# Moving the add of the shift rows in both MoE token stages from VectorE to GpSimd, and one step of ScalarE's order

## The reference, cut to what matters

```python
def rms_norm(x, g):
    xf = x.astype(jnp.float32)
    y = xf * lax.rsqrt(jnp.mean(xf * xf, axis=-1, keepdims=True) + EPS)
    return (y * g.astype(jnp.float32)).astype(x.dtype)

def modulate(h, shift, scale):
    return h * (1 + scale) + shift

for l in range(DEPTH):
    ...
    x = x + g1 * y_x                                            # after the token mixers and w_out
    hx2 = modulate(rms_norm(x, norm_ffn_g[l]), sh2, sc2)        # the token rows of this case
    x = x + g2 * grouped_moe(hx2, router_w, router_b, w_exp_gate[l], w_exp_up[l], w_exp_down[l])
    ...                                                         # the same for the context tokens in layer 0
return rms_norm(x, final_g)
```

## Time and profile before

| | |
|---|---|
| median of the runs | 1579.54 us (3 runs, 1579.3 to 1580.94) |
| profiled execution, own time | 1578.25 us |
| its span | 1576.6 us |
| TensorE busy | 1506.4 us (96%) |
| VectorE busy | 704.4 us (45%) |
| ScalarE busy | 332.8 us (21%) |
| GpSimd busy | 118.8 us (8%) |
| DMA read and written | 361.66 MB and 12.98 MB, 238 GB/s over the span |
| mean granted TensorE clock | 0.986 of full |

### The profile page before, as it was taken

How to read it: one execution, slowest core, us unless ns; L and a number is a source line. 1 busy time by engine, 2 the same in 40 slices (tenths; PEclk the granted TensorE clock), 3 DMA queues, 4 the chain that set the end, 5 groups by cost and what they waited for, 6 DMA issues and landing times. The chain is left out here.

```text
span 1576.6 us, 23833 instructions
## 1 busy us (share of the span) xinstructions
PE 1506.4 (96%) x9898; PEld 1023.3 (65%) x9898; DVE 704.4 (45%) x1420; ACT 332.8 (21%) x769; POOL 118.8 (8%) x101
## 2 busy tenths in 40 slices
PE   5999999999999999899999999999999999899995
PEld 2765644766677768775546648786678887655563
DVE  1497777577775442732221135336534312512122
ACT  2121244322223110210101023225322211100001
POOL 0100000032212210000000030000000000000000
PEclk9999999999999999999999999999999999999998
DMA  9575411333544589489999984431134376899997
GB/s 372 203 239 166 156 54 43 119 133 124 158 147 160 173 286 358 173 322 391 400 394 392 402 314 147 138 97 45 38 111 146 121 283 266 343 426 428 419 411 296
DMA packets 128364, 370.24 MB, mean 235 GB/s; under 512 B 14269, under 2 KB 91351, under 8 KB 107516
## 3 DMA queue, kind: packets, MB, share of 16 engines
q1 hardware_dynamic: 118588, 344.86, 58.8%
q10 hardware_dynamic: 5936, 13.09, 2.3%
q0 software_dynamic: 3728, 10.71, 1.9%
HBM read 361.66 MB, written 12.98 MB: 238 GB/s over the span
## 5 line engine op out<-in xcount | busy, mean ns | idle before, releaser
L1247 PE MATMUL ps<-hT,ring 128*128 128x512 f32 (+1 forms) x544 | 207.6, 535 | 0.0
L1250 PE MATMUL ps<-ring,hT 128*128 128x256 f32 (+1 forms) x832 | 173.1, 364 | 3.7 <-DVE arena L2242 2.3
L1250 PEld LDWEIGHTS ps<-ring,hT 128*128 128x128 f32 x832 | 147.0, 190 | 27.5 <-issue 10.3
L1247 PEld LDWEIGHTS ps<-hT,ring 128*128 128x128 f32 x544 | 101.3, 191 | 86.9 <-issue 81.7
L1446 PE MATMUL ps<-arena,ring 128*128 128x512 f32 (+1 forms) x384 | 136.3, 486 | 0.0
L1596 PE MATMUL ps<-arena 128*32 128x128 f32 (+2 forms) x1104 | 102.4, 342 | 0.7 <-DVE arena L2554 0.7
L1596 PE MATMUL ps<-ring,arena 128*64 128x256 f32 (+1 forms) x1280 | 93.9, 334 | 3.8 <-DMA ring<-in_w_exp_gate 2.1
L1446 PEld LDWEIGHTS ps<-arena,ring 128*128 128x128 f32 x384 | 72.4, 190 | 31.7 <-issue 24.6
L2856 POOL DMA_INDIRECT arena<-moe_rows,idx_i x23 | 22.8, 991 | 897.8 <-DVE idx_i L2622 512.9
L1381 PE MATMUL ps<-hT,ring 128*128 128x256 f32 x384 | 87.9, 379 | 0.6 <-ACT arena L1903 0.6
L1159 PE MATMUL ps<-ring,arena 128*128 128x256 f32 x384 | 85.9, 380 | 2.5 <-DVE arena L2420 2.5
(11 more groups left out here) (310 smaller groups left out, 1962.5 us busy)
## 6 DMA issues: line engine op xcount, KB each, us to landing
ring<-in_w_in SPq DMA_DIRECT2D x54, 1024.0 KB, 6.2
ring<-in_w_ada SPq DMA_DIRECT2D x48, 1024.0 KB, 5.3
arena<-in_w_exp_down SPq DMA_DIRECT2D x18, 2048.0 KB, 16.1
arena<-in_w_exp_up SPq DMA_DIRECT2D x15, 2048.0 KB, 15.8
ring<-in_w_exp_down SPq DMA_DIRECT2D x14, 2048.0 KB, 13.7
ring<-in_w_exp_gate SPq DMA_DIRECT2D x12, 2048.0 KB, 16.4
ring<-in_w_exp_up SPq DMA_DIRECT2D x12, 2048.0 KB, 15.0
hT<-in_w_exp_gate SPq DMA_DIRECT2D x10, 2048.0 KB, 15.7
```

What stands on the lines that cost most here:

```text
L1247: last = pe.matmul(ps[:, bank, 0:tok.stop - tok.start], w[:, k, at:at + width], hT[:, k, tok], start=(k == 0), stop=(k == KD - 1))
L1250: last = pe.matmul(ps[:, bank, 0:width], hT[:, k, P * tok:P * (tok + 1)], w[:, k, at:at + width], start=(k == 0), stop=(k == KD - 1))
```

## The change

GpSimd makes the adds of the shift rows: `shift_rows` moves from VectorE's list to GpSimd's, in front of the gathers of each layer. Its input no longer comes from `mix_tmp` for all tiles: the scaled rows of tile `t` go to the place of tile `t` + 1 in `h_toks`, and only those of the last tile to `mix_tmp`. VectorE counts each finished tile of scaled rows in the semaphore `consts_made` (which had stood at 4 by then), and GpSimd waits for that, and for its own add of the tile before, which reads the place that it is about to write. VectorE no longer waits for the add before `mix`; it waits for all adds of the layer only in `order_experts`, whose scratch space `by_place` begins where `mix_tmp` lies. On ScalarE `keep_parts(t - 1)` stands ahead of the squares of tile `t`, where it had stood behind them.

```diff
+CONSTS = 4
...
+        def rows_scaled(l, t):
+            return h_toks[l][:, t + 1, :] if t < NT - 1 else mix_tmp
...
                 for t in range(t0, NT):
-                    squares(ready, junk2, t, t + 1)
                     if t > t0:
                         keep_parts(t - 1)
+                    squares(ready, junk2, t, t + 1)
                 keep_parts(NT - 1)
...
                 def scale_rows(t, half):
                     cols = slice(512 * half, 512 * (half + 1))
-                    step(dve.scalar_tensor_tensor(out=mix_tmp[:, cols], in0=res[:, t, cols], scalar=rstd[:, t:t + 1],
-                                                  in1=ffn_rows[l][t // XT][0][:, cols], op0=ALU.mult, op1=ALU.mult))
-
-                def shift_rows(t):
-                    by_row = lambda a: a.rearrange("p (q k) -> p q k", k=KD)
-                    dve.tensor_tensor(h_toks[l][:, t, :].rearrange("p (k q) -> p q k", k=KD), by_row(mix_tmp),
-                                      by_row(ffn_rows[l][t // XT][1]), ALU.add).then_inc(h2_ready, 1)
+                    ins = dve.scalar_tensor_tensor(out=rows_scaled(l, t)[:, cols], in0=res[:, t, cols], scalar=rstd[:, t:t + 1],
+                                                   in1=ffn_rows[l][t // XT][0][:, cols], op0=ALU.mult, op1=ALU.mult)
+                    if half:
+                        ins.then_inc(consts_made, 1)
...
                     if v >= 2:
                         dve.wait_ge(x_mixed, v - 1)
-                    if half and t > t0:
-                        dve.wait_ge(h2_ready, before(nq, l) + t - t0)
...
                     scale_rows(t, 1)
-                    if t < NT - 1:
-                        shift_rows(t)
...
                                          op0=ALU.is_lt, op1=ALU.mult).then_inc(assigned, 1)
-                shift_rows(NT - 1)
...
                 def order_experts():
                     step(dve.tensor_tensor(versus, bc(rank[:, :].unsqueeze(1), *pair), bc(e_num.unsqueeze(2), *pair), ALU.is_equal))
                     by_number = by_place[:, 0, :, :]
+                    dve.wait_ge(h2_ready, before(nq, l + 1))
...
+            def shift_rows(l, t):
+
+                by_row = lambda a: a.rearrange("p (q k) -> p q k", k=KD)
+                if t > first_tile(l):
+                    pool.wait_ge(h2_ready, before(nq, l) + t - first_tile(l))
+                pool.wait_ge(consts_made, CONSTS + before(nq, l) + t - first_tile(l) + 1)
+                pool.tensor_tensor(h_toks[l][:, t, :].rearrange("p (k q) -> p q k", k=KD), by_row(rows_scaled(l, t)),
+                                   by_row(ffn_rows[l][t // XT][1]), ALU.add).then_inc(h2_ready, 1)
+
             for l in range(DEPTH):
                 pool.dma_start(list_d.rearrange("(p n) o -> p (n o)", p=P), no_token[:, :]).then_inc(zeroed, 16)
+                for t in range(first_tile(l), NT):
+                    shift_rows(l, t)
                 pool.wait_ge(next_idx, nth_list(l, 1))
```

More of the change, by code:

```diff
@@ L458, in trunk @@
         rows_zeroed, mods_row = sem("rows_zeroed"), sem("mods_row_ready")
-        consts_made = sem("consts_made")
+        consts_made = sem("consts_made_then_rows_scaled")
         cols_turned, cols_kept = sem("cols_turned_then_sums_of_quarters"), sem("cols_kept_then_exps_of_constants")
```

## The result

The changed kernel takes 1583.45 us (median of 11 runs, 1582.12 to 1584.54), the kernel before 1580.19 (11 runs, 1579.3 to 1580.94). The ratio is 1.0019, with a 95% interval of 1.0011 to 1.0027: **slower by about 3 us**, where 2.8 us less was forecast. The profiled execution of the changed kernel took 1584.54 us, the longest of its 11, and that of the kernel before took 1578.25, less than any of its 11 runs here; so the 6.2 us between their spans are more than the difference of the medians. The two already stand 2.5 us apart when the stage of layer 0 begins (the first product of the second half is taken up at 632.43 instead of 629.94), though nothing is changed ahead of it, and 0.9 us at that place of layer 1. I take these two offsets out where I say so. What makes them wasn't looked for.

A forecast was written before the change was run, and what follows sets the result against it. The last expert weights' DMA was taken to bound the end, TensorE the chain before. Gains of 0.8 us in layer 0 and 2.0 in layer 1 made 2.8 us off the 1579.54 median: 1576.7 us, range 1572.5 to 1581.0.

The forecast's parts named there:

- the layer 1 term: Layer 1: `first_rows` starts 1.5 us earlier, the load waiting for TensorE follows, and the weight stream gains about 2.0 us.
- rival 1: Layer 1: TensorE's 2 us idle keeps the clock low over `first_rows`, costing 2.5 us; total 1579.2 us; chance 0.2.
- GpSimd's add: Shift-row add of one tile, 1024 columns with reordered write: taken as 2.35 us, other end 3.74 us.
- rival 4: Both layers: the reordered write stretches GpSimd's add to 3.74 us; total 1580.8 us, 1583.5 with a low clock; chance 0.16.
- The hold: Chain to the choice, both layers: GpSimd's add blocks VectorE's operations reading two SBUF operands, taking about 2.2 us.
- Rival 3: Both layers: VectorE isn't held, or only for a moment, keeping about 2.2 us each; total 1572.3 us; chance 0.08.
- The tile loop's 0.93 us: First tile, once in each layer: TensorE's router no longer waits for VectorE's copy of the transposed rows, 0.93 us gained.
- ScalarE's 0.85 us: Last tile's router: kept parts copied ahead of the squares remove a wait of 1.02 us, counted as 0.85 us gained.
- The first rows of layer 0: Behind the choice in layer 0: `first_rows` starts 0.8 us earlier, passing whole to the end of the layer.
- Rival 2: Layer 0: the clock is high over `first_rows`, 3.2 us more gained; total 1573.5 us; chance 0.12.
- The hole at 1347: DMA standstill, 1347 to 1351.5 us: the load of 1351.36 goes at 1346.5 and fills it, leaving a shorter one later.
- The residual add of layer 1: Second tile, on VectorE: held by GpSimd's add, over 0.9 us long, ending about 1340.0 instead of 1340.86.

The follow-up runs named there:

- The best kernel here: Changed kernel, each layer's last-tile add back on VectorE, 18 `keep_busy` matmuls before the choice, 8 instead of 3 behind the places: 1575.13 us, ratio 0.9962.
- the run with 17: Changed kernel with each layer's last-tile add back on VectorE and 17 instead of 10 `keep_busy` matmuls in each layer: 1578.50 us, ratio 0.9982.

## Why the prediction was wrong

**The step that failed** is the layer 1 term, 2.0 us gained, and in it the words "the load after it waits for TensorE, 1.5 us earlier than 1358.99". It took the clock over `first_rows` as the kernel before has it, though the text had just worked out that the fillers now end 2 us before the choice. That case was set aside as rival 1 with a chance of 0.2 and 2.5 us. It is what happened, in both profiles of the changed kernel, and it costs 5.5 us at the release of the load: 13.1 us instead of 7.65 for the three groups, since not only the first part of the first rows but the second part and most of the first gate weights too ran at 1.2 GHz (until 1363.3). The prediction's own sign of being wrong, a clock of 0.50 over `first_rows` of layer 1, is there. With 5.5 instead of 2.5 and the rest as forecast, rival 1 would have given 1582.2 us, outside the stated range but near the measured 1583.45. The experiment with four fillers in the kernel before shows the mechanism without the change, the one with 22 in the changed kernel takes it away. Counted from where VectorE takes up the first product of layer 1's second half, the load goes after 27.92 and 27.93 us in the two profiles of the kernel before, after 32.53 and 31.20 in the two of the changed kernel, after 33.62 with four fillers in the kernel before, and after 26.31 with 22 in the changed one. That last one is 1.6 us earlier than in the kernel before, as forecast (1.5), and that kernel takes 0.20% less (0.11 to 0.28), where 0.18% was forecast. So the rest of the sum came to about the right size once the clock was high; that it agrees so closely is in part luck, since the fillers of layer 0 were changed too.

**Point by point.**

- GpSimd's add: 2.35 us taken, 2.37 measured. The reordered write costs GpSimd next to nothing (2367 ns against 2352), so rival 4 is out, which took 3.74. The ratio of the Trainium skill ("GPSIMD Engine Reference", elementwise cycle accounting), applied to VectorE's 1.94 us, would have had 3.8. The trace differs from that use of it: 2.37 / 1.94 is 1.22.
- The hold: right in kind and size (2.1 us in both layers, on a comparison of 0.2 us). Rival 3 is out. A short operation that reaches the port first does not help, as L2564 shows: the next one is held.
- The tile loop's 0.93 us: right, in both layers. ScalarE's 0.85 us: near in the profile (1.02 less 0.29 is 0.73), though as a change of its own it can't be seen in the time.
- The first rows of layer 0, forecast 0.8 us earlier: 668.66 - 666.77 less the offset of 2.49 is 0.6 earlier. The missing 0.2 are the three fillers behind the count, which at 1.2 GHz take 1.63 us instead of 0.91 and end last. The same in layer 1: 0.87 earlier instead of 1.5. This is a second, small step that failed: I let VectorE's marks end that wait and didn't look at what stands ahead of `first_rows` on TensorE's own list. It too comes from the low clock.
- Rival 2, a better clock in layer 0: not shown. The first part took 6.03 us in the first profile and 5.65 in the second, but in the kernel before it took 6.98 in one and 5.44 in the other, so the two kernels can't be told apart here.
- The hole at 1347 filled, and another in its place: right in kind, but it was to be shorter than the first, and it is 5 us. The 1.5 us from issue to the first data, part of the 2.0 us of layer 1, is too long where the queue is empty: behind the load of 1364.51 the DMA engines move nothing until 1365.4 and are at work by 1365.6, about 1 us after the issue. No run shows the 2.0 us as such, since the spans follow the load behind TensorE alone.
- The residual add of layer 1, forecast to be held to 1340.0 and to take over 0.9 us: it ended at 1340.83, which is 0.9 us earlier than before once the offset of 0.91 is taken off, as forecast (0.86), but it took 0.78 us. The end is right by luck. VectorE waited 0.89 us for TensorE's product before it, and the add started at 1340.05, when GpSimd's had only 0.25 us to go.

## What to carry to other kernels

Where an engine waits for a short chain on others, a microsecond moved off that chain isn't gained until you have looked at what TensorE does meanwhile: ten fillers took 2.48 us here with the clock high and 4.61 with it low, so the same number of them covers a wait in one execution and leaves a gap in the next. The best kernel here had them sized for 2.4 GHz and for the longest wait, on both sides of a short burst of real work. There is a price: where the clock is low, as many of them end behind the choice (by 2.1 us with 17 in the kernel before). Look at several profiles. And an operation put on GpSimd beside VectorE was not parallel to it while both read two operands from SBUF (2.33 us instead of 0.2), while VectorE's copy out of PSUM beside it took 0.68 us, against 0.67 in the kernel before: put it where VectorE works out of PSUM or waits, not beside the chain that everybody waits for.

## What the hardware showed that I had not expected

GpSimd's reordered write (neighbours 512 bytes apart) is all but free, 2367 ns against 2352, where VectorE takes 1.94 us with the same pattern and 1.22 without it. TensorE stayed at 1.2 GHz for 20.7 us in the changed kernel (1342.6 to 1363.3), although it idled for only 1.48 us of it in one piece and was otherwise close to fully busy by the page's count; in the run with 22 fillers an idle time of 1.16 us before the count cost nothing in layer 1, and 1.13 us behind it in the run with 17 did. The length of an idle time alone doesn't decide it: in layer 0 the first profile of the kernel before and that of the run with 17 fillers without the hold have the same two idle times, 0.59 and 1.21 us, and the first part of the first rows took 6.98 us in the one, whose fillers had already run partly at 1.2 GHz, and 3.81 in the other, whose fillers ran at 2.4. What does decide it wasn't settled.
